# First mixer: the differential heads' attention between the last projections, adaLN and half of the output projection between the sparse heads' attention

## The reference

```
z = h @ w_in                      # 1024 x 3368; h: adaLN shift/scale on an RMS norm of x
aq, ak, av, bq, bk, bv, iq, ik, iw = split(z)
# A, differential heads (4): two softmax maps per head
q, k = rope(rms_norm(aq, a_qn)), rope(rms_norm(ak, a_kn))
p = softmax(causal(q @ k.T / 8));  attn = p[:, :, 0] - lam * p[:, :, 1]
o_a = rms_norm(attn @ av, a_subln) * (1 - lam_init)
# B, sparse heads (8): an indexer picks 64 keys per query, attention over these
score = sum_h iw[h] * relu(iq[h] @ ik.T);  sel = top_k(score, 64)
o_b = softmax(masked(q @ k.T / 8)) @ bv          # q, k normed and roped as above
x = x + gate * (concat(o_a, o_b) @ w_out)
```

## Time and profile before

| | us |
|---|---|
| median of three runs (1480.26 to 1486.0) | 1483.24 |
| the profiled execution | 1481.32 |
| its span, first to last instruction | 1479.4 |
| PE busy | 1301.4 (88%) |
| DVE busy | 430.2 (29%) |
| ACT busy | 217.7 (15%) |
| mean granted clock of PE | 0.936 |

### The profile page before, as it was taken

How to read it: one execution, slowest core, us unless ns; L and a number is a source line. 1 busy time by engine, 2 the same in 40 slices (tenths; PEclk the granted TensorE clock), 3 DMA queues, 4 the chain that set the end, 5 groups by cost and what they waited for, 6 DMA issues and landing times.

```text
span 1479.4 us, 15114 instructions
## 1 busy us (share of the span) xinstructions
PE 1301.4 (88%) x6161; PEld 653.6 (44%) x6161; DVE 430.2 (29%) x888; ACT 217.7 (15%) x458; POOL 104.0 (7%) x127
## 2 busy tenths in 40 slices
PE   5999888899898898988967977879989898999897
PEld 2444566643343333433434435764433333343333
DVE  3265577512021211111125645262111111111112
ACT  2121431111010111101100015021010101010100
POOL 2000203000200300300000000000000000000000
PEclk8999869899999999999989997969999999999999
DMA  9987703089999999999992575307999999999993
GB/s 370 384 329 302 278 26 114 8 345 429 427 428 428 427 427 429 428 427 430 426 409 100 191 315 210 106 8 284 427 429 427 428 427 429 427 427 428 427 429 151
DMA packets 51769, 493.45 MB, mean 334 GB/s; under 512 B 4712, under 2 KB 5936, under 8 KB 20848
## 3 DMA queue, kind: packets, MB, share of 16 engines
q1 hardware_dynamic: 48816, 488.33, 79.6%
q10 hardware_dynamic: 1856, 3.20, 0.6%
q0 software_dynamic: 1024, 0.88, 0.3%
HBM read 489.24 MB, written 3.15 MB: 333 GB/s over the span
## 4 chain that ended last, share of the span: by engine, by line
PE 52%; DMA 36%; DVE 7%; issue 2%; ACT 2%; SPq 1%; DVEq 0%; POOLq 0%; POOL 0%; PEldq 0%; ACTq 0%
DMA ring<-in_moe_w 34%; PE B L741 21%; PE B L578 6%; PE A L658 4%; PE B L758 4%; PE B L533 3%; PE B L591 3%; PE B L713 2%; PE A L768 2%; DMA ring<-in_ada_w 2%; PE B L522 1%; PE B L962 1%; PE B L628 1%; DVE work L1041 1%; DVE hT L1092 1%
## 5 line engine op out<-in xcount | busy, mean ns | idle before, releaser
L741 PE MATMUL B<-ring,work 128*64 128x512 f32 x2048 | 475.1, 618 | 62.4 <-DMA ring<-in_moe_w 60.0
L741 PEld LDWEIGHTS B<-ring,work 128*64 128x64 f32 x2048 | 160.2, 142 | 339.3 <-issue 337.9
L758 PE MATMUL B<-ring,work 128*64 128x512 f32 x1024 | 231.9, 594 | 1.2 <-ACT work L1694 1.2
L1312 DVE TENSOR_TENSOR work<-work,B 64x512 f32<-64x512 f32 x64 | 68.2, 1066 | 498.1 <-ACT work L1690 497.7
L758 PEld LDWEIGHTS B<-ring,work 128*64 128x64 f32 x1024 | 76.6, 137 | 136.5 <-issue 136.5
L1690 ACT ACTIVATE work<-B 64x512 f32<-64x512 f32 x64 | 37.7, 588 | 621.2 <-PE B L741 621.2
L768 PE MATMUL A<-work 128*128 128x256 f32 x512 | 118.1, 384 | 8.9 <-DVE work L1318 8.9
L768 PEld LDWEIGHTS A<-work 128*128 128x128 f32 x512 | 94.7, 190 | 28.4 <-issue 16.9
L1910 POOL COPY work<-work 128x512 f32 x62 | 38.1, 614 | 910.4 <-PE B L741 744.5
L578 PE MATMUL B<-ring,hT 128*128 128x512 f32 (+1 forms) x224 | 93.8, 578 | 4.3 <-DVE hT L1092 3.3
L1318 DVE COPY work<-B 64x512 f32<-64x512 f32 x64 | 43.7, 683 | 117.4 <-PE B L758 117.4
(11 more groups left out here) (250 smaller groups left out, 907.6 us busy)
## 6 DMA issues: line engine op xcount, KB each, us to landing
ring<-in_moe_w SPq DMA_DIRECT2D x192, 2048.0 KB, 19.6
ring<-in_ada_w SPq DMA_DIRECT2D x24, 2048.0 KB, 17.0
ring<-in_ev_w_in SPq DMA_DIRECT2D x6, 2048.0 KB, 11.9
ring<-in_od_w_in SPq DMA_DIRECT2D x4, 2048.0 KB, 19.4
ring<-in_ev_w_out SPq DMA_DIRECT2D x2, 2048.0 KB, 7.6
ring<-in_od_w_out SPq DMA_DIRECT2D x2, 2048.0 KB, 11.6
s_tables<-hT ACTq DMA_DIRECT2D x8, 256.0 KB, 9.6
ring<-s_tables SPq DMA_DIRECT2D x1, 2048.0 KB, 24.6
```

The lines of the kernel that those rows point to most:

```text
L741: ins = pe.matmul(B5[64 * m:64 * m + 64, :], xs[:, k, :], w[:, k, :], start=(k == 0), stop=(k == KD - 1))
L758: ins = pe.matmul(B7[64 * m:64 * m + 64, :], hidTb[:, q % 2, k, :], w[:, k, 512 * m:512 * m + 512], start=(k == 0), stop=(k == KF - 1))
L1312: dve.tensor_tensor(hid[64:128, q % 2, :].rearrange("p (k q) -> p q k", k=KF), silu_a[64:128, q % 2, :].rearrange("p (q k) -> p q k", k=KF ...
```

## The change

It moves work of the first mixer; no matmul is added or removed.

- Column groups come as 6, 0, 1, 2 and then 3, 4, 5. The last three are `WOVEN`: six tiles, each in two parts of four k-steps (`project0_part`), all into B4. The first tile stands between the transposes of the two token tiles of the differential q and k, the other ten parts one after each step of the differential attention.
- The differential units run first (`A_UNITS`), their P in `htok[:, :, 512:1024]`; both token tiles of their output use B5. The sparse units (`B_UNITS`) follow, P in `hT[:, 4:8]`.
- Both index logits follow the first two projections; the norm of the differential q and k comes after the top-k on DVE, that of the sparse q and k after the differential units.
- adaLN rows 2 of layer 0 stand between the two attentions. adaLN rows 0 of layer 1 go in four parts behind the first four sparse steps, in B4; the differential heads' half of the output projection goes in four parts behind the last four steps. The sparse half comes last, with the sums of squares.
- On ACT, roots 3 and 4 stand behind the copies of the fourth projection; root 5 stands inside the differential attention; roots 6, 7 and 8 stand ahead of the copy of adaLN rows 2 and of the sparse transposes.
- DVE's S5 factors move from the projections to just ahead of the S5 matrices.
- GpSimd issues the S5 parameters before the router's.

Its core:

```diff
-IN0_ORDER = [6, 3, 4, 0, 1, 5, 2]
+IN0_ORDER = [6, 0, 1, 2, 3, 4, 5]
...
-          + [("in", 2), ("in", 3)] + [("ada", 0, j) for j in range(8, 12)] + [("in", 4), ("in", 5), ("in", 6)]
-          + [("ada", 1, j) for j in range(4)] + [("out", 1), ("out", 0)])
+          + [("in", q) for q in range(2, 7)] + [("ada", 0, j) for j in range(8, 12)]
+          + [("ada", 1, j) for j in range(4)] + [("out", 0), ("out", 1)])
...
+        prob_a = htok[:, :, 512:1024].rearrange("p u (m c) -> p u m c", m=2)
+        prob_b = hT[:, 4:8, :].rearrange("p (a b) c -> p a b c", a=2)
...
+        WOVEN = [(q, t) for q in (4, 5, 6) for t in range(TT)]
+        A_OUT_AT, ADA1_COLS_AT = 5, 6
...
+        ORDER = ["x0", "x1", "x2", "x3", "bias", "ada0r0", "ada0c0", "lam", "idx0", "idx1", "ada0r1", "ada0c1",
+                 "A0", "A1", "A2", "A3"] + [f"p{j}" for j in range(NA)] + ["ada0r2", "B0", "B1", "B2", "B3", "ada0c2"]
+        for j in range(NA + LAG_PT):
+            if 0 <= j - LAG_PT:
+                ORDER.append(f"p{NA + j - LAG_PT}")
+            if j == A_OUT_AT:
+                ORDER += ["oA0", "oA1"]
             if j == ADA1_COLS_AT:
                 ORDER.append("ada1c0")
...
+        ORDER += ["oB0", "oB1", "bt0", "bt1", "bt2", "bt3", "ct0", "ct1", "k0", "h0_0", "h0_1", "h0_2", "h0_3", "ada1r1", "ada1c1", "ada1r2", "ada1c2",
...
+            def project0_part(i, part):
+                q, t = WOVEN[i]
+                g, n = TT * q + t, n_of(0, "in", q)
+                if part == 0:
+                    if t == 0:
+                        full(n)
+                    pe.wait_ge(z_ready, g - 1 if i == 0 else g)
+                for k in range(4 * part, 4 * part + 4):
+                    ins = pe.matmul(B4[:, :], hT[:, k, P * t:P * t + P], slot8(n)[:, k, :], start=(k == 0), stop=(k == KD - 1))
+                if part == 1:
+                    ins.then_inc(proj_done, 1)
+                    if t == 1:
+                        pe.wait_ge(proj_done, g + 1)
+                        pe.nop().then_inc(slot_used, 1)
...
+                bank = (B5, (B5, B4)[t], OB[t])[s]
...
+                        s = units[j - LAG_PV][0]
+                        if s == 2 and j == LAG_PV:
                             pe.wait_ge(sig_ready, 1)
...
+                        if s == 0 and j - LAG_PV == 4:
+                            pe.wait_ge(oa_copied, 1)
+                        if s == 1 and j == LAG_PV:
+                            pe.wait_ge(oa_copied, 2)
+                        if s == 1 and j - LAG_PV == 4:
+                            pe.wait_ge(ada_copied, 1)
...
+            for q in range(4):
+                project0(IN0_ORDER[q], n_of(0, "in", q), TT * q)
+                if q == 0:
+                    tr_unit("lam", [s5row[:, :]], [(in_lam, 16 * len(LAM_PARAMS))])
                 if q == 1:
...
                     for t in range(TT):
                         tr_unit(f"idx{t}", [z0[:, t, 3072:3200], z0[:, t, 3200:3328], ikrep[:, t, :]], [(qk_ready, t + 1)])
...
                     pe.wait_ge(par_ready, 1)
                     pe.wait_ge(p5_dt, 1)
                     index_logits(0)
...
+                    ada_rows(0, 1)
+                    index_logits(1)
+                if q == 2:
+                    ada_columns(0, 1)
...
+            def qk_columns(name, col, t, ready):
+                for h in range(2):
+                    tr_unit(f"{name}{2 * t + h}", [z0[:, t, col + 512 * h + P * b:col + 512 * h + P * b + P] for b in range(4)],
+                            [(qk_ready, ready + t)])
+            qk_columns("A", 0, 0, 3)
+            for part in range(2):
+                project0_part(0, part)
+            qk_columns("A", 0, 1, 3)
+            pe.wait_ge(idx_relu, 4)
+            pe.wait_ge(z_ready, 8)
+            pe.wait_ge(tr_ev, U["A3"] + 1)
+            def rest_of_projections(j):
+                if j < 2 * len(WOVEN) - 2:
+                    project0_part(1 + j // 2, j % 2)
+            attention(0, 0, A_UNITS, rest_of_projections)
+            ada_rows(0, 2)
+            for t in range(TT):
+                qk_columns("B", 1536, t, 5)
+            ada_columns(0, 2)
+            pe.wait_ge(z_ready, 14)
+            pe.wait_ge(tr_ev, U["B3"] + 1)
+            def beside_b(j):
+                if j < 4:
+                    ada_part(B4, 1, 0, (2 * j, 2 * j + 1))
+                if j == 3:
+                    pe.nop().then_inc(slot_used, 1)
+                if j == A_OUT_AT:
                     for t in range(TT):
...
+                        tr_unit(f"oA{t}", [htok[:, t, P * b:P * b + P] for b in range(4)], [(o_ready, 1 + t)])
+                if j == ADA1_COLS_AT:
+                    tr_unit("ada1c0", [modrow[:, P * b:P * b + P] for b in range(4)], [(ada_copied, 1)])
+                if j >= NA:
+                    if j == NA:
+                        pe.wait_ge(tr_ev, U["oA1"] + 1)
+                    out_proj(0, 0, j - NA, True)
+            attention(0, NA, B_UNITS, beside_b)
             for t in range(TT):
...
+                tr_unit(f"oB{t}", [htok[:, t, 512 + P * b:512 + P * b + P] for b in range(4)], [(o_ready, 3 + t)])
+            pe.wait_ge(tr_ev, U["oB1"] + 1)
+            for b in range(4):
+                out_proj(0, 1, b, False)
...
-            set_norm(1, 6, 1536)
...
+            set_norm(0, 6, 0)
+            for j in range(NA + 1):
+                if j < NA:
+                    softmax_unit(0, j, *A_UNITS[j], sc_sb, prob_a)
+                if j:
+                    combine_unit(j - 1, *A_UNITS[j - 1][1:])
+                if j == 3 + LAG_PV:
+                    out_rows_a(0, 4)
+            set_norm(1, 12, 1536)
+            out_rows_a(1, 8)
+            for j in range(NA):
+                softmax_unit(NA, j, *B_UNITS[j], sc_sb, prob_b)
+            out_rows(NA, 0, B5, NA + 4, 512)
+            out_rows(NA, 1, B4, NA + 8, 512)
+            s5_factors()
             s5_matrices()
...
+                    if hook and base == 0:
+                        hook(j)
                     if 0 <= j - LAG_PT:
                         att_pt(base, j - LAG_PT, *units[j - LAG_PT], pt)
...
+                    if hook and base:
+                        hook(j)
...
+            for q in range(4):
...
+                    for t in range(TT):
+                        tr_evac(f"idx{t}", idxT[:, 0:3, P * t:P * t + P], 3)
+                    index_relu(0)
+                    index_relu(1)
                     ada_evac(0, "r1")
...
+                    index_relu(2)
+                    index_relu(3)
...
+            def qk_evac(name, blk, t):
+                for h in range(2):
+                    tr_evac(f"{name}{2 * t + h}", qkT0[:, blk + 4 * h:blk + 4 * h + 4, P * t:P * t + P], 4)
+            root(3, small[:, 0:16])
+            root(4, small[:, 0:16])
+            qk_evac("A", 0, 0)
+            z_evac(*WOVEN[0])
+            qk_evac("A", 0, 1)
+            def rest_of_projections(j):
+                if j % 2 == 0 and 2 <= j <= 2 * len(WOVEN) - 2:
+                    z_evac(*WOVEN[j // 2])
+                if j == 3 + LAG_PV:
+                    root(5, small[:, 0:4])
+            attention(0, A_UNITS, sc_sb, prob_a, PT, rest_of_projections)
+            for t in range(TT):
+                root(6 + t, small[:, 0:16])
+            root(8, small[:, 0:4])
+            ada_evac(0, "r2")
+            for t in range(TT):
+                qk_evac("B", 8, t)
+            ada_evac(0, "c2")
+            def beside_b(j):
+                if j == 4:
+                    act.wait_ge(ada_done, 4)
+                    act.copy(modrow[:, :], B4[:, :]).then_inc(ada_copied, 1)
+                if j == A_OUT_AT:
                     for t in range(TT):
...
+                        tr_evac(f"oA{t}", hT[:, 0:4, P * t:P * t + P], 4)
                 if j == ADA1_COLS_AT:
                     ada_evac(1, "c0")
...
+            attention(NA, B_UNITS, sc_sb, prob_b, PT, beside_b)
...
             pool.wait_ge(tr_ev, U["A3"] + 1)
             for dst, src, slow in S5_PARAMS:
                 pool.dma_start(dst, src, allow_slow_non_contiguous=slow).then_inc(in_s5, 16)
+            for dst, src, slow in ROUTER_PARAMS[0]:
+                pool.dma_start(dst, src, allow_slow_non_contiguous=slow).then_inc(in_router[0], 16)
```

More of the change, by code:

```diff
@@ L627, in att_pv, with attention @@
                     for kt in range(t + 1):
-                        ins = pe.matmul(OB[t][:, hw * h:hw * h + hw], pt[:, (base + j) % 2, m * (t + 1) + kt, :],
+                        ins = pe.matmul(bank[:, hw * h:hw * h + hw], pt[:, (base + j) % 2, m * (t + 1) + kt, :],
                                         z[:, kt, vcol + hw * h:vcol + hw * h + hw], start=(kt == 0), stop=(kt == t))
                 ins.then_inc(pv_done, 1)
-            def attention(l, base, units, hook):
+            def attention(l, base, units, hook=None):
                 n = len(units)
@@ L645, in attention, with out_proj @@
+                        if s == 1 and j - LAG_PV == 4:
```

(53 more changed lines are left out.)

160 lines of the change are left out of this document (39 added, 121 removed).

## The result

The changed kernel takes 1499.5 us (median of 4 runs, 1498.5 to 1500.5), the kernel before 1482.3 in the same comparison: the ratio is 1.0117, with a 95% interval of 1.0104 to 1.0130. It is slower by 17 us; 1496 was forecast. The profiled execution has a span of 1498.6 us (19.2 more than before), with 1303.7 us of PE busy.

What follows compares the result with a forecast made beforehand. Expert weight transfers bound the kernel, so first-mixer time counts one for one. Weaving -23.7, waits +25.0 and clock +11.3 gave +12.6 us on 1481.3, so 1493.9; the median lies 1.9 higher, say 1496, range 1480 to 1503.

Steps and rivals of the forecast that it cites:

- The bound: Expert weight transfers set the pace; time the first mixer gains or loses moves the kernel's end one for one.
- What weaving can give: Both attention stages at full clock with no new waits: 24.0 us of units for 46.4, net -23.7 us.
- The factor of 0.6: Light attention matmuls at 2.4 GHz take 0.6 of their 1.2 GHz time; bounds 0.5 and 0.8.
- Wait 1: Before the differential transposes, PE idles 6.1 us: the norm's root stands behind the last projection copy on ScalarE.
- Wait 2: Late in differential attention, PE waits 4.2 us for copies behind the output norm's root and an exp table load.
- Wait 3: Before the second sparse transposes, PE waits 7.65 us for the adaLN rows' copy, behind three roots on ScalarE.
- Wait 4: At the first sum of squares, PE waits 5.7 us for DVE's S5 factors and matrices, which lost their cover.
- The late fall in the sparse stage: Clock fall in 9 us of light matmuls between last adaLN part and output projection; costs 2.8, 2.0 us taken.
- Table loads on the path: ScalarE table loads cost about 1.3 us each; the skill page's extra drain would add 4 us over three loads.
- the clock holds: Rival: woven parts keep the clock full through the pauses, so no clock term: +1.3 us, 1484.5; chance 0.24.
- ScalarE's queue doesn't hold PE: Rival: the first three waits mostly vanish, with 6 us of clock loss: -11.4 us, 1472; chance 0.14.
- More is lost: Rival: all light sparse-stage matmuls run at 1.2 GHz, some 7 us more: 1503; within the 0.62 for slower.

Runs made afterwards that it cites:

- e3: Kernel after, with ScalarE taking the roots of the sparse q and k norms inside the last two steps of the differential attention; 1494.2 us.
- u1: e5, with the ten woven projection parts run ahead of the differential attention instead of within its steps; 1492.5 us.
- e6: Kernel after, with twelve extra unused 512-column matmuls on TensorE in its wait for the first square; 1499.3 us.
- e9: Kernel after, with six extra unused 512-column matmuls on TensorE in its wait for the first square; 1491.3 us.
- e5: Kernel after, with differential and sparse roots, S5 factors and products, and woven copy all earlier, and the differential output norm cut in two; 1461.2 us.
- e2: Kernel after, with ScalarE taking the two roots of the differential q and k norm earlier, not both behind the last projection copy; 1488.1 us.
- e1: Kernel after, with the S5 factors and twelve products on VectorE moved between the two output rows of the sparse heads; 1493.7 us.
- e4: Kernel after, with ScalarE copying the finished woven projection tile ahead of that step's exp instead of behind it; 1487.8 us.

## Why the prediction was right

The forecast was slower, 1480 to 1503 with 1496 the likeliest; it is 1499.5. By its steps:

- *The bound.* Right: what the first mixer loses arrives at the end one for one. From the first expert to the end it is 1192.5 us before, 1193.4 after and 1192.4 to 1193.5 in six of the experiments. The other four differ (1197.2 in e3, 1199.7 in u1, 1192.0 in e6, 1187.8 in e9) by what the last section tells.
- *What weaving can give.* Right in sum: -23.7 was forecast without waits and at full clock, and e5, which comes near that, is 20.0 below before (20.7 in span, 1.1 of it start-up). The factor of 0.6 holds: 9.6 to 10.6 us for the differential units, 9.6 forecast, and 14 for the sparse ones, 14.4 forecast.
- *Wait 1.* 6.1 forecast, 6.39 measured; e2 shows the cause. Its clock: 2.65 forecast, 3.0 measured.
- *Wait 2.* 4.2 forecast, 4.24 measured, in the two parts as told. Its clock: 0.9 taken, with 1.75 as the upper end; 3.0 measured, a part in 6.59 instead of 3.6.
- *Wait 3.* 7.65 forecast, 7.45 measured. Its clock: 4.0 taken, about 2.3 measured (16 transposes, the first score and the first adaLN part, against the same in e5).
- *Wait 4.* 5.7 forecast, 5.86 measured; e1 shows that the lost cover is the cause, e9 that the clock behind it comes of the pause. The clock: 1.75 taken, 3.1 measured.
- *The late fall in the sparse stage.* 2.0 taken, none came: the clock stays at 1.0 there.
- *Table loads on the path.* 1.3 us each, as taken: one starts at 164.72, and its exp at 166.01. The Trainium skill (ScalarE: Activation LUTs, What ACT_TABLE_LOAD costs) adds some 1.38 us of drain, of which no row here shows anything.
- *What was missed.* The sum has 0.3 us for the woven tiles sharing a bank. I followed the copy only to its own readiness, and not the order on ScalarE: the exp ahead of it waits for PE's transposes in the same step. 2.85 us of waits and a fall of 1.8, and e4 shows it. This is the one wait that the forecast lacks, under "Wait 1", where it says "0.3 at the second woven tile, since the woven tiles share one bank".

The two sums against each other, in the profiled execution: forecast +12.6, measured +19.2. Missed circle +4.6, clock of waits 1, 2 and 4 +3.8, clock of wait 3 and the late fall -3.7, the waits themselves +0.3, start-up +0.8, from the first expert on +0.9: 6.7 for the 6.6.

The waits were worked out and came as worked out. That the clock behind them agrees in sum (11.3 forecast, 11.4 measured) is luck: waits 1, 2 and 4 cost 3.8 us more clock than taken, wait 3 and the sparse stage 3.7 less.

The rivals: "the clock holds" failed, for the clock fell behind all four waits and behind the missed circle too, and the loss was about 13.2 us (3.0, 1.8, 3.0, 2.3 and 3.1). "ScalarE's queue doesn't hold PE" failed: waits 1 to 3 have 18.1 us. "More is lost" came about in size (4 of its 7 us), but by another mechanism than the one it named.

## What to carry to other kernels

Laying dense work between light steps buys cover and clock only if every copy and root that it depends on is placed by when its input is ready: go through the in-order programs of the helper engines, and for each instruction that stands ahead of a wanted one ask what it waits for, above all whether that is the waiting engine itself. A stage cut in two exposes the norms that used to lie beside it; find the idle time of VectorE ahead of a wait for TensorE (14.6 us here) and put what is not urgent there. A wait of 6 us among dense work costs its own length and, here, 2 to 3 us of half clock on top, so four waits of 24 us decided over a gain of 24 us.

## What the runs showed of the hardware that I had not expected

*One stage, two lengths.* From the second mixer's sums of squares to its router it takes 195 to 196 us in nine of the twelve traces, but 199.7 in e3, 200.2 in u1 and 200.0 in e6, though the program there is the same. In the three stretches of ten us from 130 us behind its first sum of squares on the clock of e3 goes 0.94, 0.50, 0.71 where that of after goes 1.00, 0.66, 1.00. 4 us is as much as an edit here, so the place where an edit acts tells more than the median.

*A wait that got shorter with more instructions ahead of it.* Behind the experts of layer 1 PE starts the sums of squares. In after and in e9:

```profile
789.73 6.16 PE L586 MATMUL B<-htok,cst 128*128 128x256 f32 x16 [9.67 <-DVE htok L1115]
```

```profile
782.37 6.10 PE L586 MATMUL B<-htok,cst 128*128 128x256 f32 x16 [5.60 <-issue]
```

The first square was ready at 784.46 in after and at 781.16 in e9: after started 5.3 us behind it, when all four were done, e9 1.2 us behind it. The idle time is 4 us shorter in both kernels with the extra matmuls (480.5 and 480.6 us from the first expert to this point, 484.3 to 485.1 in nine of the others), and all that differs in them from after is six or twelve more matmuls on PE before it. This is the other half of e9's gain. In u1, whose edit lies elsewhere, the same place has 11.78 us, also put down to "issue", and the stretch is 486.6 us. That PE's own instructions come late there is my reading of the word "issue" and was not tested.
